# Routing tables in other places, and five weight tiles of the first two experts split during routing

## The reference, cut to what matters

```python
hx = rmsnorm(x)                                   # 1056 tokens x 1024
g_logits, e_logits = hx @ w_group, hx @ w_router  # 4 groups, 32 experts
grp = argmax(g_logits);  top 2 experts inside that group, with weights
# sort the assignments by expert, 128 rows to a block
for e in experts:
    y = (silu(xb @ w_gate[e]) * (xb @ w_up[e])) @ w_down[e]   # 1024 -> 256 -> 1024
x = x + sum over the two experts of weight * y
```

## Time and profile before

| | us |
|---|---|
| median of 3 runs | 2118.3 |
| lowest, highest | 2111.08, 2120.66 |
| the profiled execution, its own time | 2127.6 |
| its span, from the first to the last instruction | 2125.9 |
| TensorE busy in it | 1843.0 |
| VectorE, ScalarE, GpSimd busy in it | 891.1, 689.8, 423.4 |

### The profile page before, as it was taken

How to read it: one execution, slowest core, us unless ns; L and a number is a source line. 1 busy time by engine, 2 the same in 40 slices (tenths; PEclk the granted TensorE clock), 3 DMA queues, 4 the chain that set the end, 5 groups by cost and what they waited for, 6 DMA issues and landing times.

```text
span 2125.9 us, 30844 instructions
## 1 busy us (share of the span) xinstructions
PE 1843.0 (87%) x11845; PEld 1677.1 (79%) x11846; DVE 891.1 (42%) x1510; ACT 689.8 (32%) x1209; POOL 423.4 (20%) x236
## 2 busy tenths in 40 slices
PE   6999999999998799999999977989899288888880
PEld 4887997988887799998999957979899267777760
DVE  5522122122122001334344434233423579889966
ACT  4322222221221121233233323121203067777752
POOL 3001102002002000000000013000003258888852
PEclk9999999999999899999999967999999689999995
DMA  5023503504505423332221134322513169999956
GB/s 166 16 85 81 105 21 86 108 19 85 115 8 83 96 81 110 118 109 68 65 68 65 53 107 161 131 95 81 165 60 120 48 237 336 328 329 334 333 188 250
DMA packets 147356, 271.84 MB, mean 128 GB/s; under 512 B 43868, under 2 KB 113820, under 8 KB 133868
## 3 DMA queue, kind: packets, MB, share of 16 engines
q1 hardware_dynamic: 111648, 210.68, 30.4%
q0 software_dynamic: 16688, 40.14, 7.3%
q10 hardware_dynamic: 18912, 19.47, 3.1%
HBM read 223.14 MB, written 65.38 MB: 136 GB/s over the span
## 4 chain that ended last, share of the span: by engine, by line
PE 75%; DVE 7%; ACT 6%; issue 6%; DMA 3%; DVEq 1%; SPq 1%; POOL 1%; another core or an unknown queue 0%; POOLq 0%; ACTq 0%; PEldq 0%
PE pb L750 17%; PE pb L751 16%; PE pb L752 16%; DVE dl L2096 3%; PE pw L942 3%; PE pq L962 3%; ACT gu1h L1193 2%; PE pb L950 2%; PE pw L857 2%; PE pw L750 2%; PE pw L752 2%; PE pw L751 2%; ACT dh L1193 1%; PE pw L846 1%; PE pq L830 1%
## 5 line engine op out<-in xcount | busy, mean ns | idle before, releaser
L750 PE MATMUL pb<-aTh,wlo 128*128 128x352 f32 x1152 | 388.1, 337 | 26.2 <-issue 12.2
L750 PE MATMUL pb<-whi,aTl 128*128 128x256 f32 (+1 forms) x1296 | 378.8, 292 | 26.1 <-ACT zo L1193 18.3
L751 PE MATMUL pb<-aTl,whi 128*128 128x352 f32 x1152 | 378.8, 329 | 2.8 <-issue 2.8
L752 PE MATMUL pb<-aTh,whi 128*128 128x352 f32 x1152 | 378.9, 329 | 0.0
L751 PE MATMUL pb<-wlo,aTh 128*128 128x256 f32 (+1 forms) x1296 | 368.6, 284 | 0.0
L752 PE MATMUL pb<-whi,aTh 128*128 128x256 f32 (+1 forms) x1296 | 366.7, 283 | 0.0
L750 PEld LDWEIGHTS pb<-whi,aTl 128*128 128x128 f32 (+1 forms) x1296 | 235.9, 182 | 42.1 <-issue 21.0
L750 PEld LDWEIGHTS pb<-aTh,wlo 128*128 128x128 f32 x1152 | 224.7, 195 | 31.6 <-issue 24.2
L752 PEld LDWEIGHTS pb<-whi,aTh 128*128 128x128 f32 (+1 forms) x1296 | 236.6, 183 | 0.9
L751 PEld LDWEIGHTS pb<-wlo,aTh 128*128 128x128 f32 (+1 forms) x1296 | 235.4, 182 | 2.1
L752 PEld LDWEIGHTS pb<-aTh,whi 128*128 128x128 f32 x1152 | 223.5, 194 | 2.9 <-issue 2.9
(11 more groups left out here) (372 smaller groups left out, 3255.3 us busy)
## 6 DMA issues: line engine op xcount, KB each, us to landing
stage<-in_w_in SPq DMA_DIRECT2D x30, 1024.0 KB, 5.6
raw<-in_w_gate_e SPq DMA_DIRECT2D x19, 1024.0 KB, 6.9
raw<-in_w_up_e SPq DMA_DIRECT2D x19, 1024.0 KB, 8.5
raw<-in_w_down_e SPq DMA_DIRECT2D x19, 1024.0 KB, 7.7
stage<-in_w_gate_e SPq DMA_DIRECT2D x13, 1024.0 KB, 6.7
stage<-in_w_up_e SPq DMA_DIRECT2D x13, 1024.0 KB, 8.4
stage<-in_w_down_e SPq DMA_DIRECT2D x13, 1024.0 KB, 8.0
zt_scratch<-zo ACTq DMA_DIRECT2D x80, 128.0 KB, 1.7
```

What stands on the lines that cost most here:

```text
L750: pe.matmul(out, ll, rh, start=first, stop=False)
L751: pe.matmul(out, lh, rl, start=False, stop=False)
L752: return pe.matmul(out, lh, rh, start=False, stop=last)
```

## The change

1. The stack `s4r` of the routing's tables moves from the place of gu1h and gu1l to that of the RMSNorm's tiles (`h2T`, `wr`, `gF`, `junk`, `rb`, `h2`, now a stack `s4n` of their own).
2. `ORDER` begins with g 0, u 0, g 1, u 1, d 0: the first down tile comes fifth (before, it was seventh, behind g 2 and u 2). From the eighth place on the list is as before.
3. ScalarE splits d 0, g 1 and u 1 high right behind u 0, ahead of the routing's Exp; before, g 1 and u 1 came after the routing and d 0 in the loop's second turn.
4. GpSimd splits d 0, g 1 and u 1 low behind u 0, ahead of its wait for the routing's end; before, VectorE did g 1 and d 0 in the loop, and GpSimd u 1.

```diff
-            s4r = ExitStack()
-            with s4r:
-                OR = r4("OR", [128, 2 * NT, 128])
...
             gu1h = a4("gu1h", [128, 2 * CHUNK], F32R)
...
             with s4a:
...
+                s4n = ExitStack()
+                with s4n:
+                    h2T = [e4(f"h2T{i}", [128, KT, 128]) for i in range(2)]
...
+                s4r = ExitStack()
+                with s4r:
+                    emp = r4("emp", [128, 2, NBLK])
...
-        ORDER = [("g", 0), ("u", 0), ("g", 1)]
+        ORDER = [("g", 0), ("u", 0), ("g", 1), ("u", 1), ("d", 0)]
+        EARLY = tuple(ORDER)
...
             main_high("g", 0)
             main_high("u", 0)
+            act.wait_ge(o_mm, 4 * NT)
+            main_high("d", 0)
+            main_high("g", 1)
+            main_high("u", 1)
             act.wait_ge(r_v, 1)
...
             x_high(0, 0)
-            main_high("g", 1)
             for e in range(NE + 2):
-                if e + 1 < NE:
-                    if e >= 1:
-                        act.wait_ge(e_gu, e)
+                if 1 <= e and e + 1 < NE:
+                    act.wait_ge(e_gu, e)
                     main_high("u", e + 1)
-                if 1 <= e <= NE:
-                    if e >= 2:
-                        act.wait_ge(e_y, e - 1)
+                if 2 <= e <= NE:
+                    act.wait_ge(e_y, e - 1)
                     main_high("d", e - 1)
...
             x_low(0, 0)
             for e in range(NE + 1):
-                if e + 1 < NE:
+                if 1 <= e and e + 1 < NE:
                     low(PLACE["g", e + 1], "g", (e + 1) % 2, e + 1)
+                if e >= 2:
+                    low(PLACE["d", e - 1], "d", 0, e - 1)
                 if e >= 1:
-                    low(PLACE["d", e - 1], "d", 0, e - 1)
                     h_low(e - 1)
...
             low("g", 0)
             low("u", 0)
+            low("d", 0)
+            low("g", 1)
+            low("u", 1)
             gp.wait_ge(r_v, R_END)
...
-                if e + 1 < NE:
+                if 1 <= e and e + 1 < NE:
                     low("u", e + 1)
```

More of the change, by code:

```diff
@@ L248, in build @@
             a4 = lambda n, s, dt=F32: alloc(s4, n, s, dt)
-            s4r = ExitStack()
-            with s4r:
-                r4 = lambda n, s, dt=F32: alloc(s4r, n, s, dt)
-                OR = r4("OR", [128, 2 * NT, 128])
[L254 to L267, removed]
             gu1h = a4("gu1h", [128, 2 * CHUNK], F32R)
@@ L282, in build @@
                 b4 = lambda n, s, dt=F32: alloc(s4a, n, s, dt)
[L283 to L288, removed]
                 LG = b4("LG", [128, NT, 8])
@@ L303, in build @@
                 big = b4("big", [128, 1])
+                s4n = ExitStack()
+                with s4n:
+                    e4 = lambda n, s, dt=F32: alloc(s4n, n, s, dt)
+                    h2T = [e4(f"h2T{i}", [128, KT, 128]) for i in range(2)]
+                    wr = e4("wr", [128, KT, 128])
+                    gF = e4("gF", [128, D])
+                    junk = e4("junk", [128, D])
+                    rb = e4("rb", [128, 36])
+                    h2 = [e4(f"h2{i}", [128, D]) for i in range(2)]
+                s4r = ExitStack()
+                with s4r:
+                    r4 = lambda n, s, dt=F32: alloc(s4r, n, s, dt)
+                    emp = r4("emp", [128, 2, NBLK])
+                    cmp8 = r4("cmp8", [128, NE, 8])
+                    Ae = r4("Ae", [128, NE, NT])
+                    cum = r4("cum", [128, NE, NT])
+                    O = r4("O", [128, 2, NT, NE])
+                    A = r4("A", [128, NT, NE])
+                    Ac = r4("Ac", [128, NT + 1, NE])
+                    R = r4("R", [128, NT + 1, NE])
+                    RO = r4("RO", [128, 2, NT, NE])
+                    cnt = r4("cnt", [128, 4, NE])
+                    cmpq = r4("cmpq", [128, 2 * NT, 8])
+                    sl = r4("sl", [128, 8, 2 * NT])
+                    cmp = r4("cmp", [1, NOVER, NE])
+                    OB = r4("OB", [128, 2 * NT, 2, NBLK])
+                    OR = r4("OR", [128, 2 * NT, 128])
             s4b = ExitStack()
@@ L2274, in low @@
                 gp.wait_ge(HI[m], e + 1)
-                gp.tensor_tensor(half(WLO, e % 2, m), rawv(PLACE[m, e], m), half(WHI, e % 2, m).bitcast(F32),
-                                 ALU.subtract).then_inc(LO[m], 1)
+                gp.tensor_tensor(half(WLO, e % 2, m), rawv(PLACE[m, e], m),
+                                 half(WHI, e % 2, m).bitcast(F32), ALU.subtract).then_inc(LO[m], 1)
             low("g", 0)
             low("u", 0)
+            low("d", 0)
+            low("g", 1)
+            low("u", 1)
             gp.wait_ge(r_v, R_END)
```

## The result

The kernel after takes 2138.78 us (median of 4 runs, 2136.36 to 2145.86), the kernel before on the same chip 2115.96: ratio 1.0114, 95% interval 1.0078 to 1.0149. That is 22.8 us slower by the medians, and between 16.5 and 31.5 by the interval. Run again later, it took 2137.09 us against 2116.89 (20.2 us; ratio 1.0087, 1.0057 to 1.0117). The forecast was slower, +12.55 us. The profiled execution has a span of 2135.6 us and a time of its own of 2137.31.

A forecast was written before the change was run, and what follows sets the result against it. TensorE held 75% of the chain of waits, but VectorE bounded the routing stretch. Routing +12.7 and loop -0.15 made +12.55 us, added to the median 2118.3: 2130.9, say 2131 us, range 2120 to 2137.

The forecast's parts named there:

- Three low splits on GpSimd: Routing: splits queued behind u 0's hold up VectorE's comparison, scaling and addition, one each; 12.7 us late, chance 0.62.
- the one-input scaling does stand still: Routing; rival said the scaling isn't held up, or the comparison slips through, so fewer stops: +9.6 us, chance 0.18.
- VectorE never got ahead: Routing; rival said VectorE gets in first and GpSimd's splits wait: not slower, -0.15, at best -1.1 us, chance 0.13.
- no split took longer than 4.54 us: Routing; rival said GpSimd's low splits take 5.19 us each, as in the loop: +14.7 us, chance 0.07.
- Three high splits on ScalarE: Routing, ahead of the Exp: some 5.5 us of splits hidden in ScalarE's 9.78 us wait for VectorE, 0 us.
- Tables and loads: Routing tables moved and loads reordered: same instructions and shapes, and no high split waiting for a load, so 0 us.
- What the loop gets back: Expert loop: splits gone from its first turns; 0.15 us gained at the start, bounds 0 and 1.1, turns staying 11.19 us.
- what would make the prediction wrong: Listed signs: L1972 to L1979 at old durations, xg cleared near 1690, much longer routing splits, or another loop period.

The follow-up runs named there:

- the kernel after without GpSimd: The kernel after with all its low splits moved to VectorE, in the routing and the loop, GpSimd only moving rows: 2081.7 us, ratio 0.9837.

## Why the prediction was right in its sign and wrong in its size

- **Three low splits on GpSimd: right.** Five splits without a break; comparison, scaling and addition at 4.40, 4.36 and 4.65 us; routing +13.1 where 12.7 was forecast. Its rivals fall: the one-input scaling does stand still, VectorE never got ahead, no split took longer than 4.54 us. The Trainium skill, "SBUF — State Buffer", section "Who interferes with whom", names tensor_scalar among the kinds that can contend; the scaling's 4.36 us, and 0.18 where no split runs beside it, agree.
- **Three high splits on ScalarE: right.** The Exp waited 17.01 us for VectorE.
- **Tables and loads: right** at 0 (0.9988 alone). Had the gathers met the early loads, they would not have been; here the last of SyncE's loads before the gathers went out at 1657.0 to 1661.9, over 30 us ahead of the clearing. In the two variants that put the early low splits on VectorE behind the routing they collided.
- **What the loop gets back: the step that failed.** It was priced at -0.15 us and measured +6.9. It ran: down(0) starts "about 1.1 us earlier", the chain between VectorE and GpSimd keeps the turn at 11.19 us, bounds "0 and the 1.1". The first half happened: the first hTl comes 0.9 us sooner after the clearing. The second hTl did stay tied to that chain (1740.65, which is 48.18 us after the clearing, 48.06 before: 0.1 later, where 0.15 sooner was forecast). But TensorE, early with down(0) and gate/up(2), then waited 2.46 us for it rather than 1.43, its clock fell to the lower level, and it lost about the microsecond it had been ahead. That made the next gate/up late, and with it the next high and low split and hTl: a long turn, the long wait again, the clock down again. First hTl to thirteenth: 141.64 us against 134.29. Of these 7.35 us the first turn's 1.05 only gives back the early start; each of the five drops of the clock adds 12.24 + 11.40 - 2 x 11.19 = 1.26, together 6.3. The rest of the 6.9, about 0.5, lies behind the last hTl. I had bounded the step as a gain that might be nothing. That the loop's phase could change stood only under what would make the prediction wrong, without a price.
- Sum: +13.1 + 6.9 = +20.0 of the 22.8 measured (20.2 the second time); what is left is within the intervals. With only the loop's step put right, the forecast would have been 12.7 + 6.9 = 19.6.

Open: what ends the alternation. In all four runs that have it there are six long waits, of which five are followed by a drop. TensorE's timeline of the kernel after, from the fifth long wait and the sixth:

```profile
1835.73 0.48 PE L754 MATMUL pq<-dh,hTl 128*128 128x512 f32 x1 [2.45 <-DVE hTl L2121]
1836.04 0.39 PE L755 MATMUL pq<-dl,hTh 128*128 128x512 f32 x1
...
1837.28 0.63 PE L754 MATMUL pq<-dh,hTl 128*128 128x512 f32 x1
...
1859.37 0.47 PE L754 MATMUL pq<-dh,hTl 128*128 128x512 f32 x1 [2.45 <-DVE hTl L2121]
1859.68 0.40 PE L755 MATMUL pq<-dl,hTh 128*128 128x512 f32 x1
1859.91 0.40 PE L756 MATMUL pq<-dh,hTh 128*128 128x512 f32 x1
```

In the kernel after the first slow matmul starts 0.3 us behind the end of the first long wait (1741.48 by 1741.17) and later each time, 1.55 us behind the fifth. Behind the sixth none is slow, and the next turn is 11.19 us. So the alternation ends with the drops, as the account would have it; why the drop moves back from one long wait to the next, and then stays away, the runs don't show. No experiment touched this, nor the single odd turns.

## What to carry to other kernels

Before moving work to an idle GpSimd, list which small VectorE instructions would run beside it: each gap between its instructions let one through, so an idle engine's work cost a whole split per instruction. An earlier start on TensorE is only a gain if what it waits for next moves too: if not, price the longer wait with the clock behind it, as rows show it. And where two engines lock each other, try giving all the work to one: it was worth 40 us here, more than any order of the loads and splits that was tried.

## What the runs showed of the hardware

- A one-input VectorE scaling of 128x36 took 4.36 us beside a GpSimd split and 0.18 without one; the MAX8 and index searches ran at their own pace beside one (0.71 us for the nine MAX8 in the kernels before and after, and 0.71 in the kernel without low splits on GpSimd).
- In the loop of the kernel after, TensorE's granted clock fell to its lower level for 3.2 to 3.6 us behind waits of 2.44 to 2.46 us, and didn't in the kernel before, whose waits there are 1.43 us or less. The drop began 0.3 us behind the first long wait and 1.55 behind the fifth; behind the sixth, of 2.45 us, there was none. Eight spare transposes in the wait kept the clock up and took about 6.4 us off the loop.
- The gathers of xg landed in 4.3 us (median) with no weight loads issued beside them (the kernel without low splits on GpSimd) and in 9.4 with three such loads at a DMA share of 1.00 (the kernel after without GpSimd).
- A low split of 128x2048 on VectorE took 2.28 us alone and 5.31 beside one of GpSimd's in the kernel after; GpSimd's took 4.48 us in the routing and 6.26 when it began during one of VectorE's.
